# Row sums for the modulation, and a norm handed out by blocks, at the start of a two-layer block kernel

## The reference, cut to what matters

```python
mod = c @ ada_w[l] + ada_b[l]                       # 1024 -> 6 x 1024
sh1, sc1, gt1, sh2, sc2, gt2 = split(mod, 6)
h = rmsnorm(x, norm1_g[l]) * (1.0 + sc1) + sh1
p = h @ w_in[l]                                     # 1024 -> 7 x 1024
xr, yr, q, k, v, ga, gb = split(p, cuts)
y_a = rg_lru(causal_dwconv(xr)) * gelu(yr)
q, k = head_rmsnorm(q), head_rmsnorm(k)             # 8 heads of 128
y_b = stick_breaking_attention(q, k, v)
x = x + gt1 * ((sigmoid(ga) * y_a + sigmoid(gb) * y_b) @ w_out)
h2 = rmsnorm(x, norm2_g[l]) * (1.0 + sc2) + sh2     # then the FFN, with gt2
```

## Time and profile before

| | |
|---|---|
| median of 3 runs | 1678.43 us (1677.64 to 1678.77) |
| the profiled execution, its own time | 1679.01 us |
| its span, first to last instruction | 1677.2 us |
| TensorE busy | 1631.8 us, 97% |
| DVE, ScalarE, POOL busy | 60%, 48%, 48% |
| mean granted clock of TensorE | 0.988 of full |
| DMA | 166.81 MB, mean 99 GB/s |

### The profile page before, as it was taken

The page is one execution under the profiler, slowest core; times in us unless marked ns, Lnnn a source line. Parts: engine busy times, 40 slices in busy tenths (PEclk is TensorE's granted clock), DMA queues, the critical chain, the costliest instruction groups (busy, mean ns, idle before and its releaser), DMA issues.

```text
span 1677.2 us, 19574 instructions
## 1 busy us (share of the span) xinstructions
PE 1631.8 (97%) x7252; PEld 1331.1 (79%) x7252; DVE 1001.8 (60%) x1172; ACT 805.3 (48%) x1010; POOL 811.4 (48%) x583
## 2 busy tenths in 40 slices
PE   3999999999999999999999999999999999999997
PEld 2778787777778888888888888888888888888885
DVE  6687898878657728616634767566337554255541
ACT  2565666666544324424352333677554444244442
POOL 2254454454645545455565454554584352453525
PEclk7999999999999999999999999999999999999999
DMA  9333332443323233233233231211132221321312
GB/s 372 126 123 127 124 116 77 138 138 100 101 82 103 90 109 100 88 125 100 90 100 95 76 107 62 73 56 57 64 99 77 63 88 55 109 88 52 100 50 76
DMA packets 46462, 166.81 MB, mean 99 GB/s; under 512 B 5152, under 2 KB 5280, under 8 KB 45856
## 3 DMA queue, kind: packets, MB, share of 16 engines
q1 hardware_dynamic: 46368, 165.57, 29.8%
HBM read 163.45 MB, written 2.10 MB: 99 GB/s over the span
## 4 chain that ended last, share of the span: by engine, by line
PE 91%; DVE 5%; ACT 1%; DMA 1%; issue 1%; POOL 1%; SPq 0%; POOLq 0%; ACTq 0%; DVEq 0%
PE lin L658 17%; PE lin L660 16%; PE lin L659 16%; PE big L659 7%; PE big L658 7%; PE big L660 7%; DVE scr L1611 1%; PE big L771 1%; PE m_o L789 1%; PE big L1076 1%; PE big L1078 1%; PE big L1077 1%; DMA scr<-ada 1%; DVE scr L1719 1%; PE m_a L964 1%
## 5 line engine op out<-in xcount | busy, mean ns | idle before, releaser
L624 POOL TENSOR_TENSOR w_lo<-raw,w_hi 128x512 fp32r<-128x512 f32 x200 | 291.5, 1458 | 622.0 <-ACT w_hi L1115 621.7
L658 PE MATMUL lin<-h_hi,w_hi 128*128 128x512 f32 x936 | 370.4, 396 | 2.1 <-POOL w_lo L627 1.9
L660 PE MATMUL lin<-h_hi,w_lo 128*128 128x512 f32 x936 | 365.4, 390 | 0.0
L659 PE MATMUL lin<-h_lo,w_hi 128*128 128x512 f32 x936 | 365.2, 390 | 0.0
L627 POOL TENSOR_TENSOR w_lo<-raw,w_hi 128x512 fp32r<-128x512 f32 x209 | 309.9, 1483 | 13.9 <-ACT w_hi L1115 13.9
L1115 ACT ACTIVATE w_hi<-raw 128x1024 fp32r<-128x1024 f32 (+1 forms) x209 | 217.6, 1041 | 203.0 <-DMA raw<-weights 52.1
L658 PEld LDWEIGHTS lin<-h_hi,w_hi 128*128 128x128 f32 x936 | 176.2, 188 | 41.1 <-issue 2.7
L659 PEld LDWEIGHTS lin<-h_lo,w_hi 128*128 128x128 f32 x936 | 176.1, 188 | 38.1 <-issue 2.2
L660 PEld LDWEIGHTS lin<-h_hi,w_lo 128*128 128x128 f32 x936 | 176.0, 188 | 37.2
L624 POOL TENSOR_TENSOR qk_hl<-raw,qk_hl 128x512 fp32r<-128x512 f32 x43 | 59.9, 1392 | 126.8 <-ACT qk_hl L1115 126.8
L658 PE MATMUL lin<-y_hi,w_hi 128*128 128x512 f32 x260 | 101.5, 391 | 0.0
(11 more groups left out here) (507 smaller groups left out, 3401.1 us busy)
## 6 DMA issues: line engine op xcount, KB each, us to landing
raw<-weights SPq DMA_DIRECT2D x245, 512.0 KB, 3.5
slab<-ada SPq DMA_DIRECT2D x32, 512.0 KB, 4.4
scr<-ada SPq DMA_DIRECT2D x16, 512.0 KB, 6.3
raw<-weights SPq DMA_DIRECT2D x10, 256.0 KB, 2.7
x<-x_t SPq DMA_DIRECT2D x2, 1024.0 KB, 6.4
out_t<-scr SPq DMA_DIRECT2D x8, 256.0 KB, 2.6
raw<-weights SPq DMA_DIRECT2D x4, 448.0 KB, 3.4
rgw<-rg_w SPq DMA_DIRECT2D x1, 1024.0 KB, 8.6
```

Of the source, the lines that this page charges most:

```text
L624: nc.gpsimd.tensor_tensor(lo[:, 0:4 * P], raw[:, s, 0:4 * P], hi[:, 0:4 * P].bitcast(F32), ALU.subtract).then_inc(w_half, 1)
L658: nc.tensor.matmul(psum_of(n), wh, hi(k), start=(k == 0), stop=False)
L659: nc.tensor.matmul(psum_of(n), wh, lo(k), start=False, stop=False)
L660: last = nc.tensor.matmul(psum_of(n), wl, hi(k), start=False, stop=(k == nk - 1))
```

## The change

Modulation: the matrix is stored the other way round, so that a chunk holds for 128 output features all 1024 inputs. DVE spreads c over the diagonal of eight 128x128 blocks, TensorE multiplies this by ones (two fp32 matmuls), and ScalarE copies the result, the row c on every partition, from PSUM to SBUF. One `tensor_tensor_reduce` per chunk then multiplies by that row and sums along it, with the bias as the sum's start, and leaves a finished column. The one-column matmuls and the additions after them go. The first 16 chunks come in the order scale 0, shift 0, scale 1, shift 1, and so on.

Norm: DVE does two row sums, then the norm of that block, then the low half of the block before. TensorE takes five units (q0, k0, v0, q1, k1) in steps: at each block it does those chunks that `LANES` makes due. v0, q1 and k1 write the three banks of `big`, and q1 and k1 have their weights in `y_hi`, `y_lo`. The first five weight tiles are loaded between the 16 chunks, and ScalarE splits them between the blocks.

Further: the constants are loaded in two parts, x with a semaphore for each half; the small decay constants on DVE stand before the chunks; three matmuls after the sum of squares and twelve before the FFN keep TensorE busy; in the pass h = 1 TensorE does v1 ahead of the scores, which wait for the copies of q1 and k1, and ScalarE copies k1 before it handles the scores.

```diff
@@ ring_plan, bank_plan, home_plan
         if h == 0:
-            units += [("q", 0, 8), ("k", 0, 8), ("v", 0, 8), ("ada", a, 8), ("ada", a + 1, 8), ("q", 1, 8),
-                      ("ada", a + 2, 8), ("k", 1, 8), ("ada", a + 3, 8), ("v", 1, 8), ("ada", a + 4, 8)]
+            units += [("q", 0, 8), ("k", 0, 8), ("v", 0, 8), ("q", 1, 8), ("k", 1, 8), ("v", 1, 8)]
+            units += [("ada", a + i, 8) for i in range(3)] + [("xr", 0, 8)] + [("ada", a + i, 8) for i in (3, 4)]
...
+TABLE = [b for k in range(DK) for b in (DK + k, k)] + list(range(ADA_FIRST, NADA))
...
+SIDE = {("v", 0): 2, ("q", 1): 3, ("k", 1): 4}
+
+LANES = ((("q", 0), (1, 2, 3, 4, 5, 6, 7, 8)), (("k", 0), (0, 2, 3, 4, 5, 6, 7, 8)),
+         (("v", 0), (0, 0, 3, 4, 5, 6, 7, 8)), (("q", 1), (0, 0, 0, 0, 3, 6, 7, 8)),
+         (("k", 1), (0, 0, 0, 0, 0, 0, 3, 8)))
@@ SP
+            sp.dma_start(cst[:, 0:NFIRST], consts[:, 0:NFIRST]).then_inc(cst_loaded, 16)
...
             for i in range(ADA_FIRST):
+                if i in (0, 2, 4, 9, 12):
+                    load_weights((0, 2, 4, 9, 12).index(i))
                 if i >= 6:
                     sp.wait_ge(ada_used, i - 5)
@@ TensorE
+            def chunk(kind, j, k):
+
+                n = UNIT[(kind, j)]
+                if k == 0:
+                    pe.wait_ge(w_split, PACK[n] + 1)
...
             for k in range(DK):
                 square(k + 1, k == 0, k == DK - 1)
-            modulation(0)
-            modulation(1)
+            keep_clock(3, lin[:, 0], c_("ones"), x[:, 0])
+            for step in range(DK):
+                pe.wait_ge(h_low, step + 1)
+                for (kind, j), due in LANES:
+                    for k in range(due[step - 1] if step else 0, due[step]):
+                        chunk(kind, j, k)
...
-                if h == 0:
-                    pair(("q", 0), ("k", 0), H, L, normed(0))
-                elif h < HEADS:
+                if h > 1:
                     unit("q", h, H, L)
-                if h == 1:
-                    unit("k", h, H, L)
+                if g == 0:
+                    unit("v", h, H, L)
                 if g >= 0:
                     pe.wait_ge(kq_normed, 2 * g + 2)
                     if g > 0:
                         pe.wait_ge(gates_read, g)
+                    else:
+                        pe.wait_ge(q_copied, 2)
+                        pe.wait_ge(k_copied, 2)
                     scores(g)
...
             norm_sum(0)
-            modulation(5)
+            keep_clock(12, m_o[:], ones_r[:], y_hi[:, 0])
@@ ScalarE
+                if k == 3:
+                    act.wait_ge(c_turned, 1)
+                    nc.scalar.activation(c_row, c_row_ps, ACT.Copy).then_inc(c_copied, 1)
...
-            split_ahead(0)
-            highs(0)
+            for k in range(DK):
+                if k in (0, 1, 2):
+                    split_ahead(0, k)
+                if k in (4, 5):
+                    split_ahead(0, k - 1)
+                high(0, k)
@@ DVE
+                v.tensor_tensor_reduce(out=src, in0=src, in1=row, scale=scale, scalar=first, op0=M, op1=AD,
+                                       accum_out=to).then_inc(ada_used, 1)
...
+            for k in range(DK + 1):
+                if k < DK:
+                    modulate(2 * k)
+                    modulate(2 * k + 1)
+                    if k == 0:
+                        dve.wait_ge(norm_rooted, 1)
+                    v.scalar_tensor_tensor(out=tmp[:, k % 4], in0=x[:, k], scalar=sm(A1 + k), in1=rstd[:],
+                                           op0=M, op1=M).then_inc(pre_h, 1)
+                    dve.wait_ge(pre_h, counted(pre_h))
+                if k > 0:
+                    e = k - 1
+                    dve.wait_ge(h_high, e + 1)
+                    v.scalar_tensor_tensor(out=h_lo[:, e], in0=tmp[:, e % 4], scalar=sm(MOD + e),
+                                           in1=h_hi[:, e].bitcast(F32), op0=AD, op1=SU).then_inc(h_low, 1)
```

More of the change, by code:

```diff
@@ L180, in bank_plan @@
         if kind in ("rv", "vn"):
+            continue
+        if (kind, j) in SIDE:
+            bank[n], before[n] = SIDE[kind, j], None
+            last[bank[n]] = n
             continue
@@ L708, in split_sum, with keep_clock @@
                 nc.tensor.matmul(m_a[:], ones_r[:], sq_r[:, 1], start=False, stop=True).then_inc(signal, 1)
+            def keep_clock(n, bank, ones, moving):
+                for _ in range(n):
+                    nc.tensor.matmul(bank, ones, moving, start=True, stop=True)
             def norm_sum(r):
@@ L1328, in _ @@
             norm_root(norm_summed, 1, D)
-            highs(1)
+            for k in range(DK):
+                high(1, k)
             for t in range(THIRDS):
```

187 lines of the change are left out of this document (93 added, 94 removed).

## The result

The changed kernel takes **1693.92 us** (median of 4 runs, 1692.12 to 1694.14), the kernel before, run beside it, 1678.56 us (1677.64 to 1678.77): a ratio of 1.009, 95% interval 1.0077 to 1.0102. It is 15.4 us slower. The forecast was 1687.5 us, with 1673 to 1697 as its range: the direction and the range hold, the size is 6 us short. The profiled execution has a span of 1692.0 us, against 1677.2.

A forecast was written before the change was run, and what follows sets the result against it. TensorE, busy for 97% of the span, was taken as the bound. The terms +13.1 + 1.8 - 5.1 - 0.7 gave +9.1 us: 1688.1 by the profiled execution, forecast 1687.5 us, range 1673 to 1697.

The forecast's parts named there:

- (1): Start, sum of squares of x: the first root, which DVE's ladder waits for, ends at 18.6 us, against 21.6 before.
- (2): DVE's alternation of row sums and norm operations: 14 sums at 1.51 us (21.1) and 15 norms at 0.79 (11.9).
- Rival B: DVE's ladder: the row sum goes at half rate, 2.5 us each; +26 us, 1704.5 us; chance 0.10.
- (3): POOL's ten tile halves beside DVE's ladder add 0.9 us each, 9.0 us; seventh low block at 60.6 us.
- rival A: Ladder not slowed: 1.32 us a row sum and nothing for POOL; -3.6 us, 1674.8 us; chance 0.17.
- (4): TensorE after the seventh block: 16 chunks, 11.2 us, plus 1 us for half clock; five units done at 72.8 us.
- (5): From q0 to head 0's scores: ScalarE waits for yr0's weights, landing at 86.2 us; scores start at 89.9.
- rival C: Before q1's copy: no wait for yr0's weights, scores 7.7 us sooner; -0.3 us, 1678 us; chance 0.11.
- (6): From scores to TensorE's turning of head 0's attention weights: turning starts at 110.9 us against 97.80, +13.1 us.
- 1.8 us for a cold clock: After the turning starts: TensorE waits some 4 us, then runs nine matmuls at half clock, +1.8 us.
- (7): Modulation columns: three groups of 16 one-column passes leave the heads, 1.70 us each, -5.1 us.
- 0.7 us of the FFN's clock: Before the FFN: twelve keep-clock matmuls may save the half clock behind a wait, 0 to 1.4 us, taken as 0.7.

The follow-up runs named there:

- e2: The changed kernel with POOL computing only 8 of 1024 columns of the first five weight tiles' low parts, leaving out needed work: 1682.89 us.
- e1: The changed kernel with the load of yr0's weights issued right behind xr0's instead of behind chunk 21: 1683.71 us.
- e4: The kernel before, keeping its own start, with the heads' 32 modulation chunks as row sums and no one-column passes there: 1673.66 us, ratio 0.9971.
- e7: e4 plus the changed kernel's twelve keep-clock matmuls between the norm sum and the FFN: 1673.54 us.
- e5: e1 with the turn of the two lin banks begun at 1 instead of 0: 1681.01 us.
- e8: e1 with the tiles of q0 and k0 split before the first root and v0's right behind it: 1680.12 us.
- e3: The changed kernel with both edits, e1's early load and e2's omission of POOL's work beside the ladder: 1672.57 us.
- e9: e5 with unit v1 behind the scores of head 0 instead of ahead of them: 1681.09 us.

## Why the prediction was right or wrong

**(1) The root.** Predicted 18.6, 21.6 in the profiled execution: TensorE's squares ran from 10.07 to 20.2 us, where I had them end at 17.2. Of these 3.0 us, 1.1 is a slip of adding: my own terms (5.5 + 3.5 + 9.3, less 1.1 and plus 1.1) give 18.3 and not 17.2. Another 1.1 is the start, which was not set by the matmuls of the row c but by x: ScalarE's first square waited for its load until 9.38, so "x there in time" was wrong. The last 0.8 is the squares' own length. I also took a single time for what scatters: kernels with this start had the root between 18.5 and 22.1.

**(2) The ladder.** I took 1.51 us for a row sum; it has 1.39 and 1.32, start to start. Over 14 sums that is 2.2 us too much, and by luck it hid most of the root's miss: the seventh low block came at 61.3, predicted 60.6. The norm operation (0.75) was right. Rival B needed 2.5 us and is refuted by every row sum of the trace. The Trainium skill's rule that an instruction with two wide SBUF sources and an accumulator runs at half throughput ("Vector Engine (DVE) Microarchitecture Reference", Points that are easy to get wrong) does not hold for this one: 1.28 to 1.35 us, the pace of the accumulation that it replaced, plus 0.08 for the read.

**(3) POOL.** 9.0 us predicted, 8.8 measured by e2 (1.78 a tile in the steps). This refutes rival A. By the rule of the Trainium skill ("SBUF — State Buffer", Who interferes with whom) all ten halves cost something, the row sums' too; the trace agrees (row sum 1.28 to 2.19, norm operation 0.75 to 1.63), though a half costs DVE 0.88 us and not the whole 1.26 that it takes alone.

**(4) TensorE behind the ladder.** Units done at 72.8 predicted, 74.39 measured: 13.1 us behind the seventh low block, where I had 12.2. The mechanism is right; the 1 us for half clock between the steps was 1.9, and in e2, where the last steps ran at full clock, the whole is 11.1, just the 16 chunks.

**(5) From q0 to the scores.** The chain was right link by link: q0's copy, the tile, DVE's sums, SyncE's queue, yr0's weights, q1's copy. Issue came at 83.8 (82.6 predicted), landing 6.0 us later and not 3.6: the earlier trace rows show a load by itself, while here three chunks (512 KB each) were issued in the 4 us ahead of it and three more loads of that size within 2 us behind it. That these made it late is likely, but was not tried by itself. Scores at 93.6, predicted 89.9. e1 shows that the wait cost 10 us, so rival C, which had it at 7.7 and the clock, would have been a true gain had the queue allowed it.

**(6) From the scores to the turning.** 21.8 us, predicted 21.0. The turning was predicted at 110.9 and stands at 115.4: 1.2 by the issue (into which the root and the units' delay had gone), 2.4 by the landing, 0.8 here, 0.1 between. The 1.8 us for a cold clock *behind* the turning did not come: TensorE's wait was 3.2 us and ended at 107.7, ahead of it, and from 115.4 to 440 us the clock was 1.00. I put that wait at the wrong place. The half clock did follow the wait, in yr0's matmuls from 109.2 to 112.6 us, and cost almost nothing there, since ScalarE's exponential was not done before 115.31 us anyway:

```profile
109.59 0.63 PE L687 MATMUL lin<-h_hi,w_lo 128*128 128x512 f32 x1
...
114.04 1.27 ACT L1307 ACTIVATE scr<-scr 128x1280 f32<-128x1280 f32 x1 [2.25 <-DVE scr L1791]
```

**(7) The columns.** 5.1 us predicted, 4.6 measured in the changed kernel and 4.3 in e4 at the last turning. The 0.7 us of the FFN's clock were not there: 0.1 by the traces, nothing by e7. I had seen that DVE paces the blocks and took half of the bound all the same.

**The step that failed** is one that the sum did not have: I followed the turning and then took the rest for equal "but for the modulation columns". The change also took three units out of the turn of the lin banks, which made the first output unit wait for ScalarE and cost 1.9 us in the changed kernel, and 3.5 in e2, where the clock fell. The order of instructions does not show this, since nothing moves there; the table that deals out the banks does.

The sum by measured terms, against 9.1 predicted: turning +17.6 in place of +13.1 and +1.8; columns -4.6 in place of -5.1; output projection +1.9 in place of 0; FFN -0.1 in place of -0.7. That is +14.8, and the spans differ by 14.8. The misses are 2.7, 0.5, 1.9 and 0.6. The forecast lay in its range by the right mechanisms of the ladder and of yr0's load, and with errors of up to 3 us in the single terms that partly cancelled.

## What to carry to other kernels

A change that hands out early work in chunks gains nothing if the engine that makes the chunks gets more to do per chunk: count where the last chunk comes, not the first. When units leave a turn of buffers, look at who now shares a buffer with whom at the far end of the kernel, even if the order there is the same. And take a change apart before judging it: of this one the row sums in the heads were worth 4.8 us (e4), and all the rest of it cost 20.

## What the runs showed of the hardware

- A wait that the trace puts down to "issue" can be a wait for another engine: at 442.6 us it was ScalarE's read of a PSUM bank, as moving the bank showed (e5).
- Pauses of one length had different effects on the clock. Behind the 1.7 us pause at the output projection the granted clock held in the changed kernel, e1 and e8 (matmuls 0.40 us) and fell to half in e2 and e3 (0.63 us, 1.6 us lost). Behind a pause of 2.2 to 2.3 us the scores took 3.84, 4.09, 3.54 and 3.43 us in e1, e3, e5 and e8 (2.32 at full clock). The seven runs of e1 went from 1680.4 to 1684.8 us; this and the root's scatter are candidates, and neither was shown to be the cause of the spread.
- A load of 512 KB with three others issued in the 4 us ahead of it and three more within 2 us behind it took 6.0 us from issue to landing; alone it took 3.6.
- Kernels with the same start had their first root up to 3.5 us apart (e2 18.5, e9 22.1). ScalarE's first square, which waited for the load of x in all of them, began 8.0 to 10.1 us in; what decides the rest was not tried.
- A custom row sum of 128x1024 with both inputs in SBUF took 1.28 us (1.34 with a third operand from small), and 2.16 to 2.19 with a POOL half beside it.
